# A fused two-model block on one core: the second chain of the recurrent mixer is started eight stages after the first in place of one

## The reference

```python
for l in range(DEPTH_2):
    u = x @ w_in[l]
    (cb, cc, ch, cg, cq, ckv, kpe, mg, rcols, rg) = _split(u, IN_SIZES)
    y_conv = _short_conv_branch(cb, cc, ch, cg, conv_w[l])
    y_mla = _mla_branch(cq, ckv, kpe, mg, ...)
    y_rwkv = _rwkv7_branch(rcols, rg, ...)
    mix = jnp.concatenate([y_conv, y_mla, y_rwkv], axis=-1)
    x = _layer_norm(DEEPNORM_ALPHA * x + mix @ w_out[l], ln_g[l], ln_b[l])
```

```python
sa = einsum('bhvk,bhk->bhv', state, a_t)
state = state * w_t + sa * b_t + v_t * k_t
y_t = einsum('bhvk,bhk->bhv', state, r_t)
```

## Time and profile before

| what | value |
|---|---|
| time, median of 3 runs | 2364.77 us (2364.74 to 2369.1) |
| the profiled execution, time | 2368.34 us |
| its span | 2366.5 us |
| PE busy | 2318.2 us (98%) |
| DVE busy | 1467.1 us (62%) |
| ACT busy | 1162.0 us (49%) |
| POOL busy | 188.6 us (8%) |
| the mixer of layer 0, from stage 0 to the first product of `pq` | 1474.18 to 1679.18 us |

### The profile page before, as it was taken

The page is one execution under the profiler, slowest core; times in us unless marked ns, Lnnn a source line. Parts: engine busy times, 40 slices in busy tenths (PEclk is TensorE's granted clock), DMA queues, the critical chain, the costliest instruction groups (busy, mean ns, idle before and its releaser), DMA issues.

```text
span 2366.5 us, 35939 instructions
## 1 busy us (share of the span) xinstructions
PE 2318.2 (98%) x14907; PEld 1938.6 (82%) x14907; DVE 1467.1 (62%) x1860; ACT 1162.0 (49%) x1644; POOL 188.6 (8%) x210
## 2 busy tenths in 40 slices
PE   8999999999999999999999999999999999999998
PEld 8777777888888888888888898878888888788886
DVE  5999965656554554454444446746765558456666
ACT  5676655644454444444434344534563546335643
POOL 5000000001000000000000001020100010301043
PEclk9999999999999999999999999999999999999999
DMA  9544465565666666666666676434746665337466
GB/s 255 182 154 159 160 205 160 163 193 178 188 187 193 184 192 187 190 192 187 190 191 189 192 223 189 130 92 124 191 125 221 188 193 151 99 100 189 143 217 201
DMA packets 305859, 416.92 MB, mean 176 GB/s; under 512 B 52936, under 2 KB 164104, under 8 KB 304928
## 3 DMA queue, kind: packets, MB, share of 16 engines
q1 hardware_dynamic: 299232, 395.63, 56.3%
q0 software_dynamic: 6144, 18.91, 2.5%
q10 hardware_dynamic: 320, 0.08, 0.0%
HBM read 406.94 MB, written 7.87 MB: 175 GB/s over the span
## 4 chain that ended last, share of the span: by engine, by line
PE 83%; DVE 9%; ACT 2%; issue 2%; DMA 2%; POOL 1%; POOLq 0%; SPq 0%; ACTq 0%; DVEq 0%
PE banks L657 81%; DVE wp_hl L1260 3%; ACT wp_hl L2021 1%; DMA first_rows<-ln_b 1%; POOL xr L2683 1%; PE banks L777 1%; POOL xr L2685 0%; DVE r_SA L1839 0%; PE banks L789 0%; DMA xt<-x 0%; DVE u_z L1616 0%; PE banks L908 0%; DMA lng<-ln_g 0%; DVE xt L1305 0%; DVE xt L1302 0%
## 5 line engine op out<-in xcount | busy, mean ns | idle before, releaser
L1260 DVE TENSOR_TENSOR wp_hl<-raw,wp_hl 128x1024 fp32r<-128x1024 f32 x740 | 913.3, 1240 | 820.3 <-ACT wp_hl L2021 819.2
L2021 ACT ACTIVATE wp_hl<-raw 128x1024 fp32r<-128x1024 f32 x740 | 782.7, 1060 | 1024.0 <-PE banks L657 1001.0
L657 PE MATMUL banks<-wp_hl,XX_hl 128*128 128x512 f32 x3840 | 893.0, 392 | 4.2 <-DVE wp_hl L1260 4.2
L657 PEld LDWEIGHTS banks<-wp_hl,XX_hl 128*128 128x128 f32 x3840 | 714.9, 188 | 160.9 <-DVE wp_hl L1260 7.5
L657 PE MATMUL banks<-XX_hl,wp_hl 128*128 128x256 f32 (+1 forms) x3584 | 631.6, 332 | 2.1 <-DVE XX_hl L1260 1.2
L657 PEld LDWEIGHTS banks<-XX_hl,wp_hl 128*128 128x128 f32 x3584 | 526.5, 191 | 72.2 <-issue 11.9
L657 PE MATMUL banks<-wp_hl,FF_hl 128*128 128x512 f32 x1056 | 240.6, 390 | 0.0
L657 PEld LDWEIGHTS banks<-wp_hl,FF_hl 128*128 128x128 f32 x1056 | 197.9, 188 | 40.9
L657 PE MATMUL banks<-wp_hl,MXa_hl 128*128 128x512 f32 x384 | 88.3, 389 | 0.0
L657 PE MATMUL banks<-wp_hl,MM_hl 128*128 128x512 f32 x384 | 88.3, 390 | 0.0
L657 PEld LDWEIGHTS banks<-wp_hl,MXa_hl 128*128 128x128 f32 x384 | 72.1, 188 | 15.0
(11 more groups left out here) (481 smaller groups left out, 1789.2 us busy)
## 6 DMA issues: line engine op xcount, KB each, us to landing
raw<-w_in SPq DMA_DIRECT2D x304, 512.0 KB, 3.9
raw<-w_out SPq DMA_DIRECT2D x96, 512.0 KB, 4.8
raw<-w_ffn_gate SPq DMA_DIRECT2D x88, 512.0 KB, 3.7
raw<-w_ffn_up SPq DMA_DIRECT2D x88, 512.0 KB, 3.7
raw<-w_ffn_down SPq DMA_DIRECT2D x88, 512.0 KB, 4.1
raw<-w_proj_attn SPq DMA_DIRECT2D x16, 512.0 KB, 5.0
raw<-w_proj_ssm SPq DMA_DIRECT2D x16, 512.0 KB, 3.9
raw<-w_uq SPq DMA_DIRECT2D x24, 256.0 KB, 4.2
```

Of the source, the lines that this page charges most:

```text
L657: return e.matmul(o, lhsT, rhs, start=start, stop=stop, skip_group_check=True)
L1260: return tt(d, src, hi, SUB)
L2021: return e.activation(o, x, func, bias=bias, scale=scale)
```

## The change

`rwkv_turns` puts stage i - 8 of chain 1, in place of stage i - 1, behind stage i of chain 0. So chain 0 goes through its stages 0 to 7 alone, the two chains then take turns, and chain 1 has its stages 19 to 26 alone. Where a chain stands alone the number of steps behind a stage comes from a new table, `RWKV_ALONE`. With the fractions carried on, chain 0 now has 2, 2, 8, 1, 2, 2, 2 and 1 steps behind its stages 0 to 7, and the last stage ends at step 84 in place of 74.

```diff
+RWKV_LAG = 8
+RWKV_ALONE = [2, 2, 8] + [1.75] * 23 + [3]
+
+
 def rwkv_turns():
 
-    for i in range(len(RWKV_SHARES) + 1):
+    n = len(RWKV_SHARES)
+    for i in range(n + RWKV_LAG):
+        shares = RWKV_SHARES if RWKV_LAG <= i < n else RWKV_ALONE
         for c in range(2):
-            if 0 <= i - c < len(RWKV_SHARES):
-                yield c, i - c, RWKV_SHARES[i - c]
+            m = i - RWKV_LAG * c
+            if 0 <= m < n:
+                yield c, m, shares[m]
```

## The result

The changed kernel takes 2395.56 us (median of 4 runs, 2391.61 to 2397.57) against 2366.89 us for the kernel before, measured beside it (4 runs, 2364.74 to 2369.1). The ratio is 1.0118, with an interval of 1.0106 to 1.013: slower by 28.7 us. The direction was foreseen; the size was put at 13.4 us, and the time lies above the range of 2367 to 2386.

The account below looks back on a forecast made before the run. PE, busy 98% of the span, was taken as the bound. Per layer 12.2 us added less 5.5 removed gave 6.7, 13.4 for both: 2378.2 us against the median of 2364.77, range 2367 to 2386.

Parts of the forecast that it names:

- the walk of the stages: Check of all 54 mixer stages, comparing DVE's arrival (2.4 us behind PE plus operations) with PE's work between.
- stage 2 (L1791): Chain 0's stage 2: PE waits 2.1 us for the reciprocal norm, with only two steps in front; called the surest term.
- L1821: Chain 0's stage 4: PE waits 1.0 us for this DVE operation, bounds nothing and 1.2.
- the halves of the convolution: Convolution on DVE delays chain 1's additions; PE waits 2.5 us before its stage 15 and 3.4 before stage 19.
- stage 23: Chain 1's stage 23, alone with one step ahead: PE waits 0.8 us.
- The norms: Before `pq`, 12 steps stand where 22 stood, DVE just full: 2.0 us added, bounds nothing and 5.
- The sum: Per layer 12.2 us of waits and gaps added and 5.5 removed: 6.7 us, or 13.4 for both layers.
- The gaps between runs: Runs of stream steps: 54 in place of 52, each new gap 0.2 us, 0.4 us added per layer.
- Faster: Rival: the added convolution waits of 2.5 and 3.4 us don't come; 2360 us, chance 0.06.
- no difference: Rival: half of the added waits are covered by each other; 2364 to 2369 us, chance 0.12.
- Much slower: Rival: norms late by up to 5 us per layer, split behind chain 1's stage 2 late too; 2385 to 2391, chance 0.14.
- Table loads: Rival: on ACT, two switches per layer late by their drain; 2381 to 2382 us, chance 0.04.

Follow-up runs that it names:

- e1: Changed kernel with idle products put in front of the three long PE waits of each layer; 2384.06 us, ratio 1.0066.
- e9: Kernel before with four idle DVE additions ahead of chain 0's addition of stage 12 in each layer; 2379.31 us, ratio 1.0051.
- e7: Changed kernel with convolution later, 4 and 6 steps behind chain 0's stages 1 and 2, bank-freeing product first in DVE's stage 3; 2368.11 us.
- e3: Changed kernel with the convolution's operations moved on DVE's queue behind chain 0's stage 24 and chain 1's stage 19; 2375.33 us, ratio 1.0029.
- e4: Changed kernel with the old table of steps everywhere, so only chain 1's lag of eight stages is left; 2395.72 us, ratio 1.0116.
- e6: Kernel before with convolution later, bank-freeing product first in DVE's stage 3, a half step moved from stage 19 to 7; 2360.9 us, ratio 0.9975.

## Why the prediction was right in its waits and wrong in its size

**The waits.** For the named terms the walk of the stages holds, layer 0: at stage 2 (L1791) 2.1 foreseen and 2.18 measured; for L1821 1.0 and 1.16; behind the halves of the convolution 2.5 and 2.57, 3.4 and 3.42; stage 23 0.8 and 0.70. The norms were put at 2.0 and are 1.36 (0.23 + 0.42 + 0.71). Two waits that the walk had as covered came: 0.57 us for `wp_hl` and 0.33 for ACT's `r_kb`. What was to go away did go. The walk is good to 0.1 us for the four waits that it works out (2.1, 2.5, 3.4 and 0.8); the 1.0 for L1821 was chosen between two bounds, and that it lies near is in part luck, as is the total, in which the norms' surplus and the two missed waits nearly cancel.

**The step that failed** is "The sum". It adds the waits at their own length and makes that the time. What a pause does to PE's clock is not in it, not even as a term costed at nothing, as the transfers and POOL are. The runs put a second charge, 1.7 us each, on five of the pauses of 2.2 us and above in the profiled execution, 8.5 us in all. e1 (clock kept, waits filled) and e9 (only a pause added) show it from both sides. The mixer took 218.0 and 216.5 us where the prediction named 212 as its sign. The row that should have told me stood in the trace of before, outside the mixer:

```profile
1864.70 2.79 PE L777 MATMUL banks<-cst,xr 128*128 128x128 f32 x12 [4.35 <-DVE xr L1989]
```

```profile
1865.00:1869.00 4.00, 3.01 (x14) 2.64 (x13) 2.29 (x4) 3.11 (x7) 0.00 (x0) 0.50 0.18 42
1869.00:1873.00 4.00, 4.00 (x22) 4.00 (x21) 0.69 (x1) 1.61 (x4) 0.00 (x0) 0.53 0.34 93
```

The pause of 4.35 us between the layers of the kernel before is followed by a clock of 0.50 and 0.53 for 8 us. All waits of the earlier trace rows are 1.5 us or shorter, with the clock at 1.00 around them, so the rows I used priced short pauses and the change made long ones. The Trainium skill ("TensorE: Matmul & The Clock Gate", HAM oscillation — how this bites in real kernels) says that idle gaps between groups of products bring the clock back to its half, and says of a kernel's start ("What's actually happening") that the number of slow products varies from run to run. The trace agrees with both, with the 0.57 and the 1.00 behind equal pauses above. But pauses of 1.90 to 2.57 us, shorter than the gaps that the page warns of, were enough here in some places, and the measurement decides.

**Terms that were mis-sized.** The gaps between runs were put at 0.4 us per layer; the busy time beyond the clock grew by 1.5 to 1.6 (e7: 200.74 for 199.13). The 1.2 us above the 0.4 stay open: the same products at the same clock in another order, and no single row accounts for it. The 2.4 us between the layers and in the tail were foreseen as nothing; they differ as much between kernels that don't touch them (the tail has 194.8 to 198.1 us in these profiles). Of them 1.8 are busy time, and both stretches contain a long pause that the kernel before has too, with the clock lower behind it in this execution: 0.67 for 0.71 in the 14 us behind the pause of 4.35 us, 0.50 for 0.57 from the tail's pause of 3.0 us to the end. Idle time grew by 12.4 us (6.4 and 6.0), where the sum has 12.6 without its gaps. With 8.5 of clock, 3.0 of other busy time and 2.4 outside that is the span's 26.3. The medians differ by 28.7, as single executions lie some 3 us to either side.

**The rivals.** "Faster" and "no difference" needed the two convolution waits to shrink; both came in full, and e3, which takes the convolution away there, shows what they were worth. "Much slower" names a time near the true one, but by another mechanism: the norms cost 1.36 us and not up to 5. Its second part did come, in layer 0 and small: the wait of 0.57 us is for the split that stands on DVE's queue behind the nine operations of chain 1's stage 2. "Table loads" left no sign. The new loads stand on ACT around Silu:

```profile
1528.24 1.28 ACT L2028 ACT_TABLE_LOAD   x1
1529.63 0.63 ACT L2028 ACTIVATE rg<-rg 128x512 f32<-128x512 f32 x1
```

The first load ends 0.11 us before the Silu, and the second starts at 1530.28, 0.02 us behind it, so no drain shows, and PE doesn't wait for chain 1's norm behind them: the only wait for L1791 in a layer is chain 0's.

## What to carry to other kernels

When a reordering is costed by waits, look at the length of each pause and not only at their sum: the pauses of 0.5 to 1.5 us in the mixers cost their own length, while the three of 2.2 to 3.4 us in layer 0 of the changed kernel, 8.2 us together, cost 13.3. Before using a table of waits as a price list, find the longest pause in the trace of the kernel before, wherever it stands, and read the granted clock behind it. And where two waits come from one long block on another engine (here six operations of the convolution on DVE), moving the block was worth more than either order of the stages that was tried: it gave 20 us in the changed kernel and was part of the version that is 6.8 us faster than before.

## What the runs showed of the hardware

Pauses of PE up to 1.5 us in the mixers, where no long one stood just before, left the granted clock at 1.00. Pauses of 2.75 us and above in and behind the mixers (2.75, 3.0, 3.4, 3.9, 4.35 and 4.5) were followed by the lower level in every profile that has them; the kernel before has two, the 4.35 us between the layers and 3.0 us in the tail. Between, length alone does not decide: 2.22, 2.32 and 2.57 us brought it in one layer and not in the other. The work lost to the lower level was 1.7 us behind most pauses of the mixers, and up to 4.5 behind the 3.9 us of e4. In e6 the shorter of two pauses brought the lower level and the longer did not; its windows behind the pause of 1.90 us in layer 0 and around the one of 2.26 us in layer 1 (2151.5 to 2153.8):

```profile
1667.00:1671.00 4.00, 3.84 (x14) 3.34 (x15) 3.05 (x6) 2.03 (x3) 0.00 (x0) 0.57 0.67 143
2150.00:2180.00 30.00, 27.74 (x197) 25.83 (x196) 19.57 (x21) 15.78 (x21) 3.92 (x8) 1.00 0.79 199
```

What else decides was not settled. Where PE has nothing to do, products whose result nobody reads keep the clock up: e1 spends 14 of them a layer and gains 11.5 us over both.
